# The weight sums of a seven-product matrix multiply, moved from GpSimd to accumulating DMAs, with another set of sums and joins

## The reference, cut to what matters

```python
D_MODEL = 1024
D_FF = 4 * D_MODEL
h = rmsnorm(x, lp['norm_ff_pre'])
x = x + rmsnorm(jnp.square(jax.nn.relu(h @ lp['w_ff1'])) @ lp['w_ff2'], lp['norm_ff_post'])
```

## Time and profile before

| | |
|---|---|
| median of 3 runs | 1140.94 us (1140.43 to 1141.2) |
| span of the profiled execution, first to last instruction | 1137.1 us |
| PE busy, share of the span | 1122.3 us, 99% |
| PEld busy | 1039.2 us, 91% |
| DVE busy | 728.0 us, 64% |
| ACT busy | 574.5 us, 51% |
| POOL busy | 253.2 us, 22% |

### The profile page before, as it was taken

The page is one execution under the profiler, slowest core; times in us unless marked ns, Lnnn a source line. Parts: engine busy times, 40 slices in busy tenths (PEclk is TensorE's granted clock), DMA queues, the critical chain, the costliest instruction groups (busy, mean ns, idle before and its releaser), DMA issues.

```text
span 1137.1 us, 20194 instructions
## 1 busy us (share of the span) xinstructions
PE 1122.3 (99%) x8160; PEld 1039.2 (91%) x8160; DVE 728.0 (64%) x1195; ACT 574.5 (51%) x1084; POOL 253.2 (22%) x211
## 2 busy tenths in 40 slices
PE   9999999999999999999999999999999999999997
PEld 8999999999779999998889988899889889989986
DVE  6465899997784645554774463574859438626845
ACT  6564666654797533344655342554237416614642
POOL 1066888871110000000000000000044025013203
PEclk9999999999999999999999999999999999999999
DMA  9453336455103543353556204214422323242152
GB/s 218 136 145 86 98 97 174 137 152 169 44 2 99 174 132 94 116 180 107 177 157 208 70 19 130 74 40 167 117 68 76 112 74 95 74 129 68 56 174 84
DMA packets 154141, 128.76 MB, mean 113 GB/s; under 512 B 15712, under 2 KB 127264, under 8 KB 153728
## 3 DMA queue, kind: packets, MB, share of 16 engines
q1 hardware_dynamic: 142560, 114.76, 34.4%
q10 hardware_dynamic: 11488, 12.70, 3.3%
HBM read 110.73 MB, written 16.84 MB: 112 GB/s over the span
## 4 chain that ended last, share of the span: by engine, by line
PE 82%; ACT 7%; DVE 4%; POOL 2%; issue 2%; ACTq 2%; DMA 1%; POOLq 0%; DVEq 0%
PE gp L2416 24%; PE gp L2822 13%; PE sp L2822 13%; PE gp L3140 6%; PE sp L3140 6%; PE gp L2899 4%; PE gp L2726 3%; PE gp L3093 2%; PE sp L3058 1%; ACT sc L1237 1%; PE sp L2726 1%; ACTq L1114 1%; PE sp L2929 1%; ACT raw L1050 1%; POOL raw L809 1%
## 5 line engine op out<-in xcount | busy, mean ns | idle before, releaser
L1663 DVE TENSOR_TENSOR wL<-wraw,wH 128x1024 fp32r<-128x1024 f32 x139 | 180.9, 1303 | 156.8 <-ACT wH L963 154.4
L963 ACT ACTIVATE wH<-wraw 128x1024 fp32r<-128x1024 f32 x139 | 146.4, 1054 | 202.6 <-PE sp L2822 46.0
L2416 PE MATMUL gp<-aH,wH 128*128 128x288 f32 (+2 forms) x800 | 173.5, 298 | 0.0
L2416 PE MATMUL gp<-aH,wL 128*128 128x288 f32 (+2 forms) x800 | 171.4, 296 | 0.0
L2416 PE MATMUL gp<-aL,wH 128*128 128x288 f32 (+2 forms) x800 | 171.2, 296 | 0.0
L911 POOL TENSOR_TENSOR comb<-wraw 128x512 f32<-128x512 f32 x12 | 16.3, 1355 | 645.2 <-DMA wraw<-in_w_ff 578.3
L2416 PEld LDWEIGHTS gp<-aH,wH 128*128 128x128 f32 x800 | 129.3, 189 | 1.9 <-issue 1.8
L2416 PEld LDWEIGHTS gp<-aL,wH 128*128 128x128 f32 x800 | 129.8, 189 | 0.0
L2416 PEld LDWEIGHTS gp<-aH,wL 128*128 128x128 f32 x800 | 129.8, 189 | 0.0
L2822 PE MATMUL gp<-wH,fH 128*128 128x512 f32 x208 | 81.2, 390 | 0.0
L2822 PE MATMUL gp<-wL,fH 128*128 128x512 f32 x208 | 80.9, 389 | 0.0
(11 more groups left out here) (549 smaller groups left out, 2839.7 us busy)
## 6 DMA issues: line engine op xcount, KB each, us to landing
wraw<-in_w_ff SPq DMA_DIRECT2D x64, 512.0 KB, 4.3
wraw<-in_w_in SPq DMA_DIRECT2D x36, 512.0 KB, 4.2
gates_scratch<-sq ACTq DMA_DIRECT2D x16, 288.0 KB, 2.2
gate<-gates_scratch SPq DMA_DIRECT2D x16, 288.0 KB, 4.2
wraw<-in_p_att SPq DMA_DIRECT2D x8, 512.0 KB, 4.2
wraw<-in_w_glu SPq DMA_DIRECT2D x8, 512.0 KB, 4.0
wraw<-in_p_ssm SPq DMA_DIRECT2D x8, 512.0 KB, 3.8
wraw<-in_w_out SPq DMA_DIRECT2D x8, 512.0 KB, 3.9
```

The lines of the kernel that those rows point to most:

```text
L963: s_.activation(halves_of(t, j)[0][:], wraw[w][:], ACT.Copy).then_inc(wh_done, 1)
L1663: v.tensor_tensor(low[:], wraw[w][:], high[:], ALU.subtract).then_inc(wl_done, 1)
L2416: last = mm(gp[:, b + h, 0:n], w[:, k, :], y[:, k, c0:c0 + n], start=(k == 0 and w is wH[s] and y is xh), stop=(k == KT - 1 and w is wL[s]))
```

## The change

The seven products are formed from other sums. Their names stay, with other contents and in the order RA0, RA1, T1, T2, T3, RB1, T4. RA0, T2, T3 and T4 of a pair now go into one bank one after the other, each added on top of what is there: ACT copies the bank out after RA0 (`p1`) and again after T2 (`p16`), DVE subtracts it from `p_5` after T3, and ACT takes it after T4 (`out_22`). T1 and RB1 share a second bank, RA1 has a third. A pair has four readings of a bank by ACT (before: two) and three by DVE (before: five).

GpSimd's four additions are replaced by four DMAs that it issues with an addition into their destination, 256 KB each. T1 starts as a copy of half of `rb`, loaded from `w_ff1` by SP into the new tile `wsum` (one buffer of 256 KB for each pair that is under way), and `ra` is added; when T1's low part is done, another block is added to the same buffer, which makes T2; when T2's low part is done, a third, which makes T4. T3 is formed in `rb` itself. SP loads pair p+2 when the low part of T4 of pair p is done. Four semaphores of an early stage are folded into one that counts.

```diff
-        PRODUCTS = ("RA0", "T2", "T1", "RA1", "T3", "RB1", "T4")
+        PRODUCTS = ("RA0", "RA1", "T1", "T2", "T3", "RB1", "T4")
...
                     if p >= 2:
-                        sp.wait_ge(wl_done, operand_at(q, p - 2, "RB1"))
-                        sp.wait_ge(comb_ready, comb_at(q, p - 2, "T4"))
+                        sp.wait_ge(wl_done, operand_at(q, p - 2, "T4"))
...
                     sp.dma_start(pair_raw(p)[j % 2][:], src).then_inc(w_loaded[raw_slot(t)], 16)
+                    if j % 2:
+                        sp.dma_start(operand_source(p, "T1"), src[:, 0:4, :]).then_inc(w_loaded[raw_slot(t)], 16)
...
-                g.tensor_tensor(block("T3"), rb[:, 4:8, :], rb[:, 0:4, :], ALU.subtract).then_inc(comb_ready, 1)
...
+                g.dma_start(operand_source(p, "T1"), ra[:, 0:4, :], accum_op=ALU.add).then_inc(chain_added[p % 2], 16)
+                if n:
+                    pool.wait_ge(*added_at(*pair_of(n - 1), "T3"))
+                g.dma_start(operand_source(p, "T3"), rb[:, 4:8, :], accum_op=ALU.add).then_inc(t3_added, 16)
+
+            def second_sum(n):
+
+                q, p = pair_of(n)
+                pool.wait_ge(wl_done, operand_at(q, p, "T1"))
+                g.dma_start(operand_source(p, "T2"), pair_raw(p)[1][:, 4:8, :], accum_op=ALU.add).then_inc(chain_added[p % 2], 16)
+
+            def third_sum(n):
+
+                q, p = pair_of(n)
+                pool.wait_ge(wl_done, operand_at(q, p, "T2"))
+                g.dma_start(operand_source(p, "T4"), pair_raw(p)[0][:, 4:8, :], accum_op=ALU.add).then_inc(chain_added[p % 2], 16)
+
+            for n in range(0, 12, 4):
+                first_sums(n)
+                second_sum(n)
+                for i in range(n, n + 3):
+                    first_sums(i + 1)
+                    third_sum(i)
+                    second_sum(i + 1)
+                third_sum(n + 3)
...
+                    if name == "T2":
+                        pe.wait_ge(*kept_at(q, p, "p1"))
+                    if name == "T3":
+                        pe.wait_ge(*kept_at(q, p, "p16"))
+                    if name == "RB1":
+                        pe.wait_ge(*kept_at(q, p, "p5"))
+                    if name == "T4":
+                        pe.wait_ge(*join_at(q, p, "21"))
...
-                                      start=(name not in ("RA1", "RB1", "T4") and k == 0 and w is wH[i] and y is yH),
+                                      start=(name in ("RA0", "RA1", "T1") and k == 0 and w is wH[i] and y is yH),
```

More of the change, by code:

```diff
@@ L437, in build @@
         x2_back = sem("x2_back")
-        comb_ready = sem("comb_ready")
+        chain_added = [sem(f"chain_added{i}") for i in range(2)]
+        t3_added = sem("t3_added")
         sum_ready = sem("sum_ready")
@@ L487, in raw_uses @@
         def raw_uses(t):
-            return sum(raw_slot(i) == raw_slot(t) for i in range(t + 1))
+            return sum(1 + (i >= T_FF + 16 and (i - T_FF) % 16 in (1, 3, 5, 7)) for i in range(t + 1) if raw_slot(i) == raw_slot(t))
         def slot_free(t):
             return w_count(max(i for i in range(t) if raw_slot(i) == raw_slot(t)) + 1)
-        PRODUCTS = ("RA0", "T2", "T1", "RA1", "T3", "RB1", "T4")
-        OPERANDS = ("T2", "T1", "RA", "T3", "RB1", "T4")
+        PRODUCTS = ("RA0", "RA1", "T1", "T2", "T3", "RB1", "T4")
         def seven_done(n):
@@ L1562, in operand_h, with keep @@
                 else:
-                    act.wait_ge(gemm_done, g_count(T_FF + 16 * q - {"RA": 3, "T1": 2, "T3": 2, "T2": 1, "T4": 1, "RB1": 0}[name]))
+                    act.wait_ge(gemm_done, g_count(T_FF + 16 * q - {"RA": 3, "T2": 2, "T4": 2, "T1": 1, "T3": 1, "RB1": 0}[name]))
                 i, k0, k1 = operand_place(p, name)
                 s_.activation(wH[i][:, k0:k1, :], operand_source(p, name), ACT.Copy).then_inc(wh_done, 1)
+            def keep(q, p, name):
+                product, dst, bank, use = {"p1": ("RA0", p_1, 0, "12"), "p16": ("T2", p_16, 0, "11"),
+                                           "p5": ("T1", p_5, 2, "21")}[name]
+                act.wait_ge(gemm_done, product_at(q, p, product))
+                if 4 * q + p > 4:
+                    act.wait_ge(joined, join_at(q, p, use)[1] - 3)
+                s_.activation(dst[:], PAIR_BANK[p % 2][bank], ACT.Copy).then_inc(kept, 1)
@@ L2214, in _, with pair @@
             rows_l(1, 3, 5)
[L2216 to L2217 removed]
+            def pair(j):
+                return PAIR[FF1_PAIR[j]][:, :, 0:HT]
             def evac_unit(q, c, n):
@@ L3148, in ff1 @@
                     for j in range(4, 8):
-                        begin(q, j)
-                        parts(q, j, range(KT))
+                        begin(j)
+                        parts(j, range(KT))
                     return
```

283 lines of the change are left out of this document (133 added, 150 removed).

## The result

The changed kernel takes 1181.99 us (median of four runs, 1180.38 to 1183.51) against 1141.07 us: 1.0358 of the time before, 95% interval 1.0346 to 1.0371, or 41 us more. The forecast was 1161 with a range to 1195: slower was right, the size was half of what came, and the time lies where the first rival (the DMA chain paces the pairs, above 1172) had put it.

A forecast was written before the change was run, and what follows sets the result against it. PE's own matmul list was taken to bound FF1. Stalls at T3 from ACT's copy, ACT's list and late DMAs summed to 6.6 us a quarter, 20 us: 1157.1 of span, 1161 us measured, range 1150 to 1195.

The forecast's parts named there:

- the first rival: FF1's pairs paced by three dependent DMAs per buffer: 1175 at 4.4 us landing, 1210 at 6.6; chance 0.25, shared with GpSimd's list.
- Bound and gains: FF1: PE alone paces and keeps 336 matmuls a quarter; only 1.0 us of small gaps winnable, dropping GpSimd's sums worth nothing.
- Term 1: At T3, PE must wait for ACT's copy `p16`: 0.78 us for each of 12 pairs, 9.4 us.
- Term 2: ACT's list ahead of `p16` makes middle pairs stall 1.21 us; 4.0 us a quarter, 12 us in all, with DMAs free.
- Term 3: Accumulating DMAs (landing 3.75 us, hold 1.0) make T4 late, so `p16` too: 6.6 us a quarter instead of 4.0.
- the straight line: An accumulating DMA's landing, interpolated by bytes between a 2.2 us store and a 4.4 us slab load: 3.1 us.
- The bounds beside the forecast: Totals for other landings and GpSimd holds: 1153 (2.2, 0.37), 1175 (4.4, 1.44), 1210 (6.6, 1.0); loads 1 us different, 1157 to 1167.
- The list: Signs of being wrong in FF1: stalls ahead of T1, T2 or RA0, T3 without a gap, or granted clock below 1.00.
- DMA engines at 0.28, no queue busy: Argument for the rival that FF1's DMAs are hidden and only ACT's list counts: 1153, or 1150; chance 0.11.
- The clock: Sign of being wrong: granted clock below 1.00 in FF1's windows, which no part of the forecast counted.
- GpSimd held till landing: Rival: each DMA holds GpSimd's list until it lands, 22 us a quarter, 1207; chance 0.25, shared with the DMA chain.
- matmuls getting quicker: Rival: without GpSimd's traffic PE's matmuls go from 0.133 to 0.120 us apart, 13 us gained, 1140; chance 0.07.

The follow-up runs named there:

- pool_third: Changed kernel with the four sums made by GpSimd's in-place additions instead of DMAs, and T4's sum ahead of the next pair's T1 and T3: 1151.12 us.
- filler: Changed kernel plus 16 dummy matmuls into an unused bank ahead of the wait for `p16` in the second and third pair of each quarter: 1184.67 us.
- third_first: Changed kernel, DMAs kept, with GpSimd issuing T4's DMA ahead of the next pair's T1 and T3 (first pair unchanged): 1182.2 us.
- t4_pool: Changed kernel with only T4's sum made by GpSimd's in-place addition; T1, T2, T3 stay DMAs, same order: 1179.72 us.
- short_products: Changed kernel leaving out 4 of the 12 matmuls of RA1, RB1 and T4 in each pair: 1179.4 us.
- t2_early: Changed kernel, DMAs kept, with T4 first in GpSimd's list, T2 one place earlier on PE and `p16` ahead of RA on ACT: 1200.72 us.

## Why the prediction was right in direction and half in size

**Bound and gains: right.** Nothing came off PE, FF2 is as it was, the stage before ends at 845.2 us against 843.2 (843.2 to 846.6 in the other runs, which don't change it), and giving up GpSimd's sums won nothing.

**Term 1: right.** A bare hand-over at T3 was put at 0.78 us; it is 0.75 in the first pairs of the changed kernel (PE's first row below: 48 matmuls and the wait lie between 955.84 and 962.94) and in first and last pairs of `pool_third`.

**Term 2: right, a little high.** 1.21 us for the middle pairs, 4.0 a quarter, 12 in all, 1153 if the DMAs cost nothing; `pool_third` has 1.06, 3.6 a quarter, and is 10.7 us above before.

**Term 3 failed in its size: 8 us were forecast for the DMAs, 31 came.** The mechanism was as described: T4 waits in GpSimd's list for the next loads, lands late, and holds ACT's `p16`. The walk stands against quarter 2, in us after FF1's first matmul (at 955.84):

| step | forecast | measured |
|---|---|---|
| T4's low part of the first pair; SP may load | 6.9 | 6.8 |
| T2's low part of the second pair | 12.7 | 15.8 |
| loads of the third pair there | 13.2 | 15.2 |
| T4 of the second pair issued | 15.2 | 16.8 |
| it has landed | 19.0 | 21.9 |
| T3 of the second pair starts | 21.0 | 23.8 |
| SP may load the fourth pair | 20.4 | 23.3 |
| T4 of the third pair has landed | 32.5 | 38.1 |
| T3 of the third pair starts | 34.5 | 40.0 |
| FF2 starts | 51.2 | 59.3 |

Two of its durations were too short, both for one reason: a transfer was priced as if alone. The loads took 8.3 us instead of 6.3, and the landing 5.2 instead of 3.75 (GpSimd's hold was below my 1.0: issues follow each other after 0.54). The 6.0 us of the earlier trace rows are loads that have the DMA engines to themselves, and I gave the accumulations one landing whatever ran beside them. Alone a DMA takes 3.2 to 3.3 us, within my bounds and near the 3.1 of the straight line; beside T1 and T3 5.2, beside slab loads 6.2 to 6.7. So I weighed one transfer's size where the count of transfers in flight decided. FF2 starts 8.1 us late; 5.5 of these are the two turns, and the rest lies behind the third pair's T3: 0.9 at the last pair's T3 and some 1.6 of matmuls at the lower clock, which `filler` shows to be hardly a loss of their own.

The bounds beside the forecast don't all follow from the steps as written: with a landing of 4.4 and a hold of 1.44 these give some 9.7 us a quarter, 1170, where the text has 11.3 and 1175.

The estimate of 2.6 us from the Trainium skill, "DMA: Bandwidth & Descriptors", Anatomy of one DMA, is below even the lone DMA's 3.24 us here.

**Besides the clock, one more sign of being wrong came.** The list has stalls ahead of T2, and T2 of the second pair waits 0.7 to 1.1 us for `p1`, which no term counts. T2's own DMA, issued beside the third pair's loads, takes 6.7 us; ACT's copy of it waits, and `out_22`, the squares and `p1` stand behind that copy:

```profile
962.94 0.37 PE L3152 MATMUL sp<-sumH,wH 128*128 128x288 f32 x1 [0.59 <-ACT p L1590]
...
970.27 0.63 ACT L1581 ACTIVATE wH<-wsum 128x512 fp32r<-128x512 f32 x1 [3.17 <-DMA wsum<-wraw]
...
973.65 0.37 PE L3152 MATMUL gp<-sumH,wH 128*128 128x288 f32 x1 [0.91 <-ACT p L1590]
```

**The first rival was what happened, and I had its condition wrong.** I let the chain decide from a landing of 4.4 us on, and for one chain. My own walk already had a turn of 13.5 us (6.9 to 20.4), longer than PE's 11.9 a pair, so it had described a paced stage and called it a stall of PE. The name did not change its sum; the durations did. Measured, the turn is 16.5 us, and a second loop through T2 and ACT's list has 15.4. That two loops lie about 1 us from each other is why cutting either gained next to nothing (`third_first`, `t4_pool`), and why PE's work could shrink or grow without effect (`short_products`, `filler`).

**"DMA engines at 0.28, no queue busy" misled.** That was a mean over a stage; a loop with waits in it needs its transfers to be quick while they run.

**The clock** fell, as the list of what would make the forecast wrong had it, but the filler shows it to be an effect of the stalls with next to no price here. The other rivals (GpSimd held till landing; matmuls getting quicker) did not occur: issues return after half a microsecond, and without GpSimd's additions the 48 matmuls ahead of a first pair's T3 still take 7.10 - 0.75 = 6.35 us, 0.132 each.

## What to carry to other kernels

When a compute instruction is replaced by a DMA, walk the loop that it joins once around (buffer free, load, sum, split, buffer free) and compare its period with the bound engine's work for the same stretch; if it is longer, that period is the forecast, not a stall per hand-over. Price each transfer with those that are in flight beside it. If cutting one loop brings nothing, look for a second one of nearly the same length before giving up its explanation, and change the duration of one suspect (here the loads) to see all loops move at once.

## What the runs showed of the hardware

The same 256 KB accumulating DMA within SBUF took 3.24 us alone, 5.2 with two others just ahead, 6.2 to 6.7 beside slab loads (and up to 8.0 in `t2_early`). After the stalls of 2.9 to 4.4 us in the changed kernel the mean granted clock of the next 3.4 us was 0.50 to 0.71, at the lower of its two levels (1.2 GHz) for all or part of it, although PE was busy throughout. After the 1.06 us waits of `pool_third` it stayed at 1.00. Behind `filler`'s matmuls, with 1.1 to 3.6 us of waiting left after them, it stayed at 1.00 at three of six places and was 0.51 to 0.73 at the others. Windows of the changed kernel, the stall and what follows:

```profile
975.60:979.68 4.08, 0.00 (x1) 0.03 (x1) 3.23 (x5) 2.36 (x5) 0.00 (x0) 1.00 0.46 77
979.68:983.10 3.42, 3.42 (x16) 3.42 (x17) 0.73 (x2) 0.59 (x1) 0.86 (x1) 0.58 0.75 208
```
